# A fourth rounded weight tile, weight tiles split mid-chunk, and three pieces of side work put elsewhere in the order

## The reference, cut to what matters

```python
# layer 1: attention (8 dense heads, 8 windowed heads with a sink; 2 + 2 key/value heads)
h = rmsnorm(x, pre_g) * (1 + scale) + shift          # shift, scale, gate = silu(c) @ mod_w + mod_b
proj = h @ w_in                                      # queries | keys, values | gate input z
y = concat(dense(q, k, v), window(q, k, v, sink)) * silu(z)
x = x + gate * rmsnorm(y @ w_out, post_g)

# layer 2: multiscale pooling of proj in 4 groups, each times its pool_w, times silu(z); then w_out as above

# layer 3: 8 stick-breaking heads and 8 heads of chunkwise retention
h = rms_norm(x, norm_gain) * (1 + scale) + shift
q_sb, k_sb, v_sb, z_sb, q_r, k_r, v_r, z_r = split(h @ w_in)
oa = stick_breaking(norm(q_sb), norm(k_sb), v_sb) * silu(z_sb)
ob = head_group_norm(retention(rotary(q_r), rotary(k_r) / sqrt(128), v_r)) * silu(z_r)
x = x + gate * (concat(oa, ob) @ w_out)
```

## Time and profile before

| | us |
|---|---|
| median of 3 runs (lowest, highest) | 2598.04 (2596.53, 2602.52) |
| profiled execution, own time | 2595.46 |
| its span | 2593.6 |
| TensorE busy | 2528.2 (97%) |
| VectorE busy | 1617.3 (62%) |
| ScalarE busy | 958.3 (37%) |

### The profile page before, as it was taken

The page is one execution under the profiler, slowest core; times in us unless marked ns, Lnnn a source line. Parts: engine busy times, 40 slices in busy tenths (PEclk is TensorE's granted clock), DMA queues, the critical chain, the costliest instruction groups (busy, mean ns, idle before and its releaser), DMA issues.

```text
span 2593.6 us, 29840 instructions
## 1 busy us (share of the span) xinstructions
PE 2528.2 (97%) x11859; PEld 2027.7 (78%) x11859; DVE 1617.3 (62%) x2424; ACT 958.3 (37%) x1529; POOL 105.1 (4%) x115
## 2 busy tenths in 40 slices
PE   7999999999999999999999998999999999999998
PEld 4789777777777877888888887887788777787786
DVE  4456666677776758677776757356466477656432
ACT  4222434434454333332334333355455423233321
POOL 0000000000000103000000102000000000000000
PEclk8999999999999989999999998999999999999999
DMA  9945433444425745666645654323222255532342
GB/s 349 340 163 187 125 111 114 122 124 133 133 90 169 241 150 171 195 203 207 207 146 194 239 176 141 93 79 90 74 87 83 77 164 160 172 93 82 122 146 73
DMA packets 292877, 390.58 MB, mean 151 GB/s; under 512 B 11698, under 2 KB 221234, under 8 KB 288898
## 3 DMA queue, kind: packets, MB, share of 16 engines
q1 hardware_dynamic: 286608, 354.79, 43.0%
q0 software_dynamic: 6128, 33.89, 3.4%
q10 hardware_dynamic: 2, 0.00, 0.0%
HBM read 371.85 MB, written 16.78 MB: 150 GB/s over the span
## 4 chain that ended last, share of the span: by engine, by line
PE 91%; DVE 4%; DMA 2%; ACT 1%; issue 1%; SPq 1%; POOL 0%; ACTq 0%; POOLq 0%; DVEq 0%
PE G L1962 77%; PE S L1962 6%; PE OB L1962 5%; PE TB L1965 2%; PE TB L1962 1%; DMA MORE<-in_ev_mod_w 1%; DMA MRAW<-in_ev_mod_w 1%; DVE Y L1473 1%; DVE TT L1473 1%; SPq L1019 0%; PE OB L1965 0%; DVE WLO L1473 0%; DMA LATE<-in_ev_mod_w 0%; DVE HLO L1479 0%; DVE SQ L1479 0%
## 5 line engine op out<-in xcount | busy, mean ns | idle before, releaser
L1962 PE MATMUL G<-HHI,WHI 128*128 128x512 f32 x2624 | 1088.9, 415 | 28.5 <-issue 7.7
L1962 PE MATMUL G<-HHI,WLO 128*128 128x512 f32 x2624 | 1031.2, 393 | 0.0
L1962 PE MATMUL G<-HLO,WHI 128*128 128x512 f32 x2624 | 1028.3, 392 | 0.0
L1473 DVE TENSOR_TENSOR WLO<-RAW,WHI 128x1024 fp32r<-128x1024 f32 x376 | 459.2, 1222 | 282.5 <-ACT WHI L1139 279.4
L1139 ACT ACTIVATE WHI<-RAW 128x1024 fp32r<-128x1024 f32 x376 | 394.8, 1054 | 583.1 <-PE G L1962 543.7
L1962 PEld LDWEIGHTS G<-HHI,WHI 128*128 128x128 f32 x2624 | 497.2, 189 | 139.2 <-issue 23.5
L1962 PEld LDWEIGHTS G<-HHI,WLO 128*128 128x128 f32 x2624 | 495.9, 189 | 108.4
L1962 PEld LDWEIGHTS G<-HLO,WHI 128*128 128x128 f32 x2624 | 498.0, 190 | 104.8 <-issue 8.1
L1479 DVE SCALAR_TENSOR_TENSOR MACC<-MWIDE,SC,MACC 128x512 f32<-128x512 f32 x420 | 321.3, 765 | 39.5 <-DMA MWIDE<-in_od_mod_w 13.5
L1962 PE MATMUL G<-WHI,HHI 128*128 128x512 f32 (+1 forms) x384 | 145.0, 378 | 3.9 <-ACT K L1139 3.0
L1962 PE MATMUL G<-WLO,HHI 128*128 128x512 f32 (+1 forms) x384 | 136.4, 355 | 0.0
(11 more groups left out here) (274 smaller groups left out, 2346.8 us busy)
## 6 DMA issues: line engine op xcount, KB each, us to landing
RAW<-in_w_in SPq DMA_DIRECT2D x128, 512.0 KB, 3.7
MWIDE<-in_od_mod_w SPq DMA_DIRECT2D x96, 512.0 KB, 4.2
MWIDE<-in_w_ada SPq DMA_DIRECT2D x96, 512.0 KB, 4.5
RAW<-in_ev_w_in SPq DMA_DIRECT2D x80, 512.0 KB, 3.8
RAW<-in_od_w_in SPq DMA_DIRECT2D x64, 512.0 KB, 3.9
MWIDE<-in_ev_mod_w SPq DMA_DIRECT2D x32, 512.0 KB, 3.9
RAW<-in_ev_w_out SPq DMA_DIRECT2D x32, 512.0 KB, 3.6
RAW<-in_od_w_out SPq DMA_DIRECT2D x32, 512.0 KB, 3.5
```

Of the source, the lines that this page charges most:

```text
L1473: return e.o.tensor_tensor(o, a, b, op)
L1962: return e.o.matmul(o, l, r, start=start, stop=stop, skip_group_check=True)
```

## The change

1. The ring of rounded tiles gets a fourth place. No memory is left for a tile of its own, so it lies over the scratch tiles `TA` outside the stick-breaking heads (`WHI_TA`) and over the not yet written Y[14] and Y[15] during them (`WHI_Y`). `whi(i)` says which tile chunk i has. Stages that use the shared places get waits: the first split in Y waits for the reads of the layer before's Y, and so on.
2. Splits run up to i + 3 and are placed in the middle of chunk i, after its second step (`split_ahead`), instead of up to i + 2 at its end. In `gemm_dual` they are placed before `next(tiles)` of the chunk's first half.
3. `first_splits` is put at the head of the list of side tasks (`insert(0, ...)`).
4. In `ret_task` the V of each head pair is centred in a step of its own: for even n at the task's start, for odd n as an event of the task before.
5. In the last task head 15's turns lie as events between head 14's stages, the y splits 12 to 15 lie at steps 5, 7, 20 and 28, and `rt_z` waits for its own head's k alone.

```diff
     LATE = [place(f"LATE{i}", [P, 4, 256], F32, h0 + 4 * SEQ * (KT + 8 + 2 * i))[0] for i in range(4)]
-    NR, NS = 5, 3
...
     RAW, WLO = [], []
...
+    WHI3 = [place(f"WHI{i}", [P, 4, 256], F32R)[0] for i in range(3)]
     MRAW, MWIDE = [], []
...
+    WHI_TA = scratch("WHITA", [P, 4, 256], F32R, 46 * K1)
+    WHI_Y, _ = place("WHIY", [P, 4, 256], F32R, y0 + 4 * SEQ * 14)
...
 
+    stick0, stick1 = first_chunk[third + 2], first_chunk[third + 16] + 4
+    fourths = range(3, len(chunks), 4)
+    last_ta = max(i for i in fourths if i < stick0)
+    first_y = min(i for i in fourths if i >= stick0)
+    last_y = max(i for i in fourths if i < stick1)
+    next_ta = min(i for i in fourths if i >= stick1)
+
+    def whi(i):
+
+        if i % 4 < 3:
+            return WHI3[i % 4]
+        return WHI_Y if stick0 <= i < stick1 else WHI_TA
+
     nat = [("c", 0), ("c", 1)] + [("x", i) for i in range(4)]
...
+        def split_ahead(i):
+            while at["split"] < min(i + NS, len(chunks)):
+                split_next()
+
...
                     reduce_pending()
-                while at["split"] < min(i + NS, len(chunks)):
...
+                        if nt == 0 and jj:
+                            split_ahead(i)
...
                         put("mm2", "h", layer, u, i, c % 2, c // 2 * 4, nt, jj, (first + c) % 2)
+                    if jj == 0:
+                        split_ahead(i)
                     next(tiles, None)
                 used(i)
-                while at["split"] < min(i + NS, len(chunks)):
-                    split_next()
             for _ in tiles:
...
+                background.insert(0, first_splits(1))
                 at["hold"] = True
...
         def ret_task(n):
-            put("v3_centre", n)
             put("decay", 2 * n)
-            for i in range(2):
+            if n % 2 == 0:
+                yield
+                put("v3_centre", n)
+                yield
+            for i in range(2 if n < 7 else 1):
                 for what in "qk":
                     for half in range(2):
                         put("turn3", (what, 2 * n + i), half)
                         yield
-                    yield
-            if n < 7:
-                yield
-                yield
+                    if n < 7:
+                        yield
             events = {}
+            if n == 7:
+                for x in range(4):
+                    events[2 * x + 1] = [("turn3", ("qk"[x // 2], 15), x % 2)]
+            if n % 2 == 0:
+                events[13] = [("v3_centre", n + 1)]
+            if n == 7:
+                for k, t in ((12, 5), (13, 7), (14, 20), (15, 28)):
+                    events.setdefault(t, []).append(("y_split", 3, k, h_unit))
             for i in range(2):
                 h, t = 2 * n + i, (20 if n < 7 else 10) * i
                 for kt in range(4):
@@ -902,10 +937,9 @@
                 events.setdefault(t + (15 if n < 7 else 14), []).append(("rt_norm", h))
             for _ in timed(events):
                 yield
-            if n == 7:
-                for k in range(12, KT):
-                    put("y_split", 3, k, h_unit)
-                    yield
+            if n < 7:
+                yield
+                yield
 
         reduce_pending()
         at["hold"] = True
...
-                cp(WHI[i % NS][:, :, :], RAW[i % NR][:, :, :]).then_inc(*a_whi.up(i))
+                if i == first_y:
+                    e.wait_ge(spill, 3)
+                    e.wait_ge(v_tile, (3, KT - 1))
+                elif i == next_ta:
+                    e.wait_ge(p_cum, (7, 0))
+                    e.wait_ge(v_st, (7, 0, "ls"))
+                    e.wait_ge(v_st, (7, 0, "lo"))
+                cp(whi(i)[:, :, :], RAW[i % NR][:, :, :]).then_inc(*a_whi.up(i))
...
-                if (h, kt) != (0, 3):
+                if (h, kt) == (0, 3):
+                    e.wait_ge(p_gemm, last_ta)
+                else:
...
+                if layer == 3 and k >= 14:
+                    e.wait_ge(p_gemm, last_y)
...
-                e.wait_ge(v_nr, (("k3", h | 1), "end"))
+                e.wait_ge(v_nr, (("k3", h), "end"))
```

More of the change, by code:

```diff
@@ L104, in build @@
     LATE = [place(f"LATE{i}", [P, 4, 256], F32, h0 + 4 * SEQ * (KT + 8 + 2 * i))[0] for i in range(4)]
-    NR, NS = 5, 3
+    NR, NS = 5, 4
     RAW, WLO = [], []
@@ L110, in build @@
         WLO.append(place(f"WLO{i}", [P, 4, 256], F32R, at)[0])
-    WHI = [place(f"WHI{i}", [P, 4, 256], F32R)[0] for i in range(NS)]
+    WHI3 = [place(f"WHI{i}", [P, 4, 256], F32R)[0] for i in range(3)]
     MRAW, MWIDE = [], []
@@ L272, in build @@
     units += out_units(T["od_w_out"][0])
+    third = len(units)
     for p in range(4):
@@ L457, in work @@
                     put("mt", layer, u, i, c, t, pair, last, t == tiles - 1)
+                    if t == tiles // 2 - 1:
+                        split_ahead(i)
                     step(background)
@@ L469, in work @@
                     put("mw", layer, u, i, c, t, (first + t // 2) % 2, last, t == 3)
+                    if t == 1:
+                        split_ahead(i)
                     step(background)
@@ L683, in make_plan @@
                 h_unit = at["unit"]
-                background.append(first_splits(1))
+                background.insert(0, first_splits(1))
                 at["hold"] = True
@@ L823, in make_plan @@
                     h_unit = at["unit"]
-                    background.append(first_splits(2))
+                    background.insert(0, first_splits(2))
                 u, pair = gemm("h", 2)
@@ L949, in make_plan @@
                 h_unit = at["unit"]
-                background.append(first_splits(3))
+                background.insert(0, first_splits(3))
             u, pair = gemm("h", 3)
@@ L1578, in dve_program @@
                 e.wait_ge(a_whi, i)
-                tt(WLO[i % NR][:, :, :], RAW[i % NR][:, :, :], f(WHI[i % NS][:, :, :]), SUB).then_inc(*v_wlo.up(i))
+                tt(WLO[i % NR][:, :, :], RAW[i % NR][:, :, :], f(whi(i)[:, :, :]), SUB).then_inc(*v_wlo.up(i))
             elif stage == "mod_acc":
@@ L2032, in pe_program @@
                 i = k // 4 * 2 + (0 if what == "k" else 1)
-                wh, wl, j = WHI[i % NS], WLO[i % NR], k % 4
+                wh, wl, j = whi(i), WLO[i % NR], k % 4
                 hi, lo = HHI[:, k, :], HLO[:, k, :]
@@ L2062, in pe_program @@
                 kind, layer, u, i, c, nt, jj, pair, last = a
-                wh, wl = WHI[i % NS], WLO[i % NR]
+                wh, wl = whi(i), WLO[i % NR]
                 cols = slice(nt * P, nt * P + P)
@@ L2125, in pe_program @@
                 layer, u, i, c, t_, pair, last, final = a
-                wh, wl = shaped(WHI[i % NS], 2), shaped(WLO[i % NR], 2)
+                wh, wl = shaped(whi(i), 2), shaped(WLO[i % NR], 2)
                 o, cols = G[pair][t_ % 2][:, :], slice(t_ * P, t_ * P + P)
```

## The result

The changed kernel took 2586.77 us (median of 5 runs, 2584.44 to 2591.96) against 2598.76 (5 runs, 2596.53 to 2602.52) for the kernel before: ratio 0.9951, 95% interval 0.9935 to 0.9966, so 9 to 17 us faster. Forecast were 2583 and a range of 2573 to 2594. The profiled execution took 2586.77 with a span of 2584.8.

A forecast was written before the change was run, and what follows sets the result against it. TensorE, busy 97% of the span, was taken as the bound, so its waits counted. A to F summed to 14.3 us, taken as 14.0: 2581.5 from the profiled run, 2584.0 from the median, 2583 predicted, range 2573 to 2594.

The forecast's parts named there:

- A: y splits first in the step, at 785.21: TensorE's 2.90 us wait for HLO falls to 1.0, gain 1.9, bounds 0 and 2.9.
- B: Earlier splits, at 1815.93 and one like it: K copy waits fall from 1.52 to 0.57, gain 1.9, bounds 0 and 3.0.
- C: Centring and ring, at 2164.36: the 3.39 us WLO wait with its clock goes, 5.7, two short ones 1.7; sum 7.4.
- D: Last unit of w_in: 13.1 us of old losses go, a new 3.4 us wait for K and others come; gain 5.4.
- E: Passages between layers: a WLO of 1.14 us now stands uncovered ahead of the sum, twice; -2.3, bounds -2.5 and 0.
- F: Everywhere else: splits moved by a half chunk may hit softmax rows or leave them; 0, bounds -2 and +2.
- One reading in the prediction: Half clock after the 3.87 us wait was read as its effect; 2.3 us counted for each wait of 3.39 and more.
- R1: Rival: every wait goes and none comes, D gives 13.1 and E 0; 24.3 us gained, 2573 us; chance 12%.
- R2: Rival: waits only move, D gives 0, A's gain is lost, attention loses 2; 2593 or 2590.5 us; chance 15%.
- R3: Rival: splits ahead of the softmax in attention delay TensorE by 1.0 us per row; 2616 us; 6% with other losses.
- R4: Rival: the ring does nothing, WLO as late as before, C gives 4.7 and B nothing; 2588 us; chance 12%.

The follow-up runs named there:

- experiment 8: Changed kernel with the first y splits appended behind the head's task again, in all three layers: 2589.88 us (1 run).
- experiment 4: Changed kernel with a ring of three rounded tiles instead of four, splits still mid-chunk: 2581.55 us, ratio 0.9932 to the kernel before.
- 5: Kernel before with only the side work's edits, ring of three and splits at the chunk's end: 2585.83 us, ratio 0.9945.
- 6: Changed kernel with V's centring put back at each task's start, behind the norm's chain: 2598.97 us (1 run).
- e_append: Kernel of experiment 8: changed kernel with the first y splits behind the head's task again, 2589.88 us.
- e_end3: Kernel before with only the side work's edits, ring of three and splits at the chunk's end: 2585.83 us.
- experiment 1: Changed kernel with tile SM 64 bytes shorter, which moves the scratch area and the fourth tile to a multiple of 128: 2580.45 us, ratio 0.9925.
- e_combo: Changed kernel with ring of three, scratch area on a multiple of 128 and gemm_dual's splits behind next(tiles): median 4.4 us lower, 8 us by the ratios.
- 7: Changed kernel with its last task as before: 2600.90 us with earlier scores also waiting for both heads' k, 2594.96 us without that wait.
- e_align: Kernel of experiment 1: changed kernel with the scratch area moved to a multiple of 128, 2580.45 us.
- e_mis_before: Kernel before with its three rounded tiles moved 64 bytes off a multiple of 128: 2612.02 us (2 runs), ratio 1.0047.
- e_best3: e_combo with two idle steps ahead of head 14's events in the last task: 9.6 us less than e_combo in the medians, 5.0 in the trace.
- e_last_clean: Changed kernel with the last task alone as before, only scores of heads 14 and 15 waiting for both heads' k: 2594.96 us (1 run).
- e_last_old: Changed kernel with the last task as before and earlier heads' scores also waiting for both heads' k: 2600.90 us (1 run).

## Why the prediction was right

The time lay in the range, 3.8 us above the forecast. Point by point:

- *A*, HLO of k = 11. Shown by experiment 8. The size was off: 3.2 gained for 1.9, above the bound of 2.9. I had left 1.0 us of wait, for a Y that VectorE would finish late behind an added WLO; there is none. The later softmax, costed at nothing, did cost nothing.
- *B*, K copies. 0.58 is left of 1.52, forecast 0.57. Shown by experiments 4 and 5, at both places.
- *C*. Right in sum, 5.1 + 1.4 for 5.7 + 1.7. A second wait came in view, MACC at 2176.68, 1.3 for 0.3: VectorE's delay in the norm's chain is still there and now meets another reader. The clock that went with the long wait was also worth more: 0.54 in the mean over 6 us, so 2.8 lost where I had 2.3. Of the causes that I named, either suffices for the long wait, the side work's edits (5) or the earlier splits with four tiles (6), but each leaves a MACC wait of 2.5 or 4.2 in its place; the half chunk is needed for the short ones (4, 5). The fourth tile does nothing for any of them (4).
- *D*. The wait for K was 3.73 against 3.4, with 0.50 behind it, and the HLO 2.11 against 2.0. The gain was 6.8 against 5.4. Most of the difference is the clock: the stretch at 0.50 that went cost 2.8, and the new one 1.7 (mean 0.72 over 6 us), where I had 2.3 for both. The addition of slots in the order's sequence holds: VectorE's rows in the kernel after follow one another as counted, from the HLO at 2359.38 to the end of K's turn, 8.2 us against 7.9.

```profile
2359.38 0.69 DVE L1516 TENSOR_TENSOR HLO<-Y,HHI 128x512 fp32r<-128x512 f32 x1
...
2364.72 1.40 DVE L1516 TENSOR_TENSOR TT<-K,SN 64x512 f32<-64x512 f32 x2
...
2366.88 0.69 DVE L1516 TENSOR_TENSOR K<-K,TT 128x512 f32<-128x512 f32 x1
```

- *E*. 1.5 us of wait at each passage against 1.14: I had priced VectorE's slot and forgotten that its operand comes from ScalarE, whose rounding stands behind the gate as well. With what follows (the HLO wait at 1580 grew from 1.8 to 2.5) the two cost 3.3, forecast 2.3.
- *F* is the step that failed in size: "0, bounds -2 and +2", costed as what a moved split may hit. One of 64 softmax rows was hit, by 0.58 (PB, at 768; it is there in e_append and not in e_end3, so it is the mid-chunk split). But the new tile's address slowed the matmuls that use it outside attention, some 8 us (experiment 1), above my bound. I had looked at what the tile holds and who waits for it, and not at where it lies.
- *The wait for KTA* is in no part. The fourth tile removed it, 2.3 us (experiment 4).

Without the address's 8 us the ledger's 7.2 would be about 15, for a forecast of 14.3. The medians' 12.0 is the ledger's 7.2, 1.5 more ahead of the 160th us (KTA's 2.3, less what the waits for the modulation's weights took back), and 3.3 by which the profiled execution of before lay below its median of 5 runs. So the mechanism of parts A to E was right, but that the time came within 3.8 us of 2583 is in part luck: a loss of 8 us that I had not seen was in part made good by gains that I had not counted.

One reading in the prediction does not carry what it was used for. The 0.50 behind the 3.87 us at 973.55 is no effect of that wait: from 965 to 968 us, ahead of it, the clock was 0.50 already. The waits of 3.39 and 4.5, which began at clock 1.00, do bear it out.

R1 and R2 are excluded by the new wait for K and by D's gain, R3 by the attention phase (+0.8), R4 by the waits for WLO. The clock behind the new wait of 3.73 us was 0.50, but behind the same wait in e_combo it was 1.00; behind waits of 2.90 (before), 3.00 (experiment 8) and 3.12 (7, at 2382) it was 1.00, and behind 2.14 (e_align) 0.50. By the Trainium skill, "TensorE: Matmul & The Clock Gate", section "HAM oscillation — how this bites in real kernels", idle time puts the clock back to half. It had the changed kernel's new wait right, but these traces show both outcomes for waits of nearly the same length.

## What to carry to other kernels

Where TensorE is busy all the time, idle time is not the only loss: compare how many matmuls stand in equal windows, or the start of the same matmul in both traces. When a buffer is put over other memory, look at its address beside its hazards: here 64 bytes took 8 us of the 15 that the rest brought in the ledger. When two single traces differ by 2 or 3 us, look at the clock behind each wait before you give the difference to the edit. And a wait that goes tends to be one work item on another engine (here 2.4 us of centring) standing in the wrong place; where it is moved, ask who now stands behind it, on the engine that makes its operand as well.

## What the runs showed of the hardware

- A matmul of 128x512 with a rounded float32 tile as stationary operand started 227 ns after the one before (1000 to 1550 us, kernel before). With one tile in four 64 bytes off a multiple of 128 (changed kernel), those with this tile took 235 and 230 ns, and those between them 234; with all three tiles of a ring off (e_mis_before), 230.5, 229.0 and 227.7. With the scratch area on a multiple of 128 (e_best3), matmuls whose moving operand lies in it (the pooled tiles PHI and PLO) took 227 as well, where in the kernel before PHI x WHI took 232, PHI x WLO 229 and PLO x WHI 226.
- Past the 160th us, of 16 waits of 3.39 us or more that began at clock 1.00 (all fourteen traces together), 15 were followed by 0.50 (1.2 GHz) and one, of 3.73 in e_combo, by 1.00 (2.4 GHz). Shorter ones went either way: 1.78 was followed by 1.00 in the kernel before and by 0.50 in five others, 2.11 by 1.00 and 2.14 by 0.50, 3.12 (e_last_clean) by 1.00 and 3.13 (e_last_old) by 0.50, 3.27 by 1.00 (e_mis_before, twice). A stretch at 0.50 behind such a wait lasted 3 to 6 us and cost half of that.
